# Two arenas of on-chip memory move up by 32 bytes in each partition

## The chip, the cores and the metric

The kernel runs on one core of one Trainium2 chip. The time is device microseconds of one execution, from its own launch to its end. Three runs of the kernel before took 1703.72, 1704.83 and 1706.70 us, a median of 1704.83 us. One further execution was recorded by the hardware profiler; all rows below are of that one.

## The reference

The reference chains two blocks over a sequence of 512 tokens of width 1024, all in 32-bit floats, and returns the normalised stream.

```
def reference(x, c, ctx, ..., g_final_2):
    x = first_block(x, c, ctx, ...)           # modulated norm, 10,240-column projection, 8x64 neighbourhood
                                              # attention with 256 context keys, gated convolution, merge
    return second_block(x, mem_2, ...)        # differential + forget-gate causal attention, memory
                                              # cross attention, squared-ReLU MLP of 4,096, final norm

y_a = (silu(z_a) * b_gate * _dwconv3(c_gate * x_in, conv_w, conv_b)) @ w_out_conv
y_b = (silu(z_b) * attn_o) @ w_out_attn
merged = sigmoid(g_a) * y_a + sigmoid(g_b) * y_b          # then  merged @ w_o
...
a = relu(h @ w1);  (a * a) @ w2                           # the MLP of the second block
```

Almost all arithmetic is matrix products of 1024-wide activations with weight matrices.

## The kernel before, in words

Every weight matrix is cut into jobs of 1,024 x 256 elements (129 of them, 1 MB each). The tensor `raw` holds two jobs as they arrive from memory. ACT copies a job to `wh`, which rounds it to the shortened 32-bit type (fp32r in the rows; `split_hi`, line 314), and DVE or POOL writes what the rounding lost to `wl` (`split_job`, line 320). A product is then three matmuls (`mm3`, lines 438 to 440): high weights with high activations, high with low, low with high. Two such buffers alternate, and the queue of SyncE loads the next job once both parts of the one before last are made.

Activations lie in two arenas, which are two tensors that the whole kernel cuts into views by hand, in KB from the arena's start (`F` and `R`, lines 115 to 120): `farena`, 29.5 KB in each partition, for plain 32-bit values (accumulated results, masks, the residual stream), and `rarena`, 128 KB, for the rounded operands of TensorE in high and low parts. Four further names, `early`, `late`, `upper` and `crown`, are plain 32-bit windows over parts of `rarena`: each is allocated and released again, so that its address stays with the region that `rarena` then takes (lines 93 to 104).

Three kinds of products follow from this. In the usual one (`tiles_job`, `mm3`) a 128x128 piece of `wh` or `wl` is the stationary operand and 512 or 256 columns of `rarena` move through. Where the result is wanted with tokens in the partitions (`token_group`, lines 516 to 518) it is the other way round: a piece of `rarena` is stationary, and 256 columns of `wh` or `wl` move. Where a block product with seven instead of eight multiplications is used (`seven`), the sums of weight quadrants lie in `rarena` too, so that for three of the seven products both operands are in `rarena`; and attention has both operands in the arenas as well. The rows name the moving operand first: `acc<-rarena,wh` moves `rarena` over a stationary `wh`, `acc<-wh,rarena` moves `wh` over a stationary `rarena`, and `acc<-rarena` has both there.

The order of the work is written out by hand engine by engine, with semaphores between them. No planner and no scheduler has a say.

Addresses come from the order of the allocations. The first, `raw`, starts at byte 16,512 of a partition, which is 129 x 128. `raw`, `wh` and `wl` take 16,384 bytes each; `par` 516 bytes, which the allocator rounds up to 544; `ident` and `ones` 512 each; `small` (176 values, line 89) 704. `farena` then starts at 67,936 = 530 x 128 + 96, and, 30,208 = 236 x 128 bytes further, `rarena` at 98,144 = 766 x 128 + 96. All views in the arenas that TensorE reads start a multiple of 256 bytes from the arena's start.

Of the kernel before, what the change touches and what calls it, by code (L numbers as in the profile page):

```python
# [70 lines left out]
def build(nc, A, out):  # L71
# [3 lines left out]
    with ctx:  # L75
        def sb(name, shape, dt=f32):
            return ctx.enter_context(nc.sbuf_tensor(name, shape, dt))
# [8 lines left out]
        par = sb("par", [128, NPAR])  # L86
        ident = sb("ident", [128, 128])
        ones = sb("ones", [128, 128])
        small = sb("small", [128, 176])
        F_KB, R_KB = 29.5, 128  # L90
        farena = sb("farena", [128, int(F_KB * 256)])

# [2725 lines left out]
```

How the kernel before makes its waits and increments, by code:

```python
    def link(self, ins):  # L51
        self.n += 1
        ins.then_inc(self.sem, 1)
        self.eng.wait_ge(self.sem, self.off + self.n)
# [198 lines left out]
        def W(eng, name, value):  # L253
            if not (isinstance(value, int) and value <= 0):
                eng.wait_ge(s_(name), value)
# [11 lines left out]
        def hold(eng, name, value):  # L267
            eng.wait_ge(s_(carried[name][0]), value + carried[name][1])
# [41 lines left out]
        def split_hi(act, it, per, base):  # L310
            s = base % 2
            act.wait_ge(s_(f"raw_loaded{s}"), half(it, per, base) * 16 + 16)
            nc.scalar.activation(wh[:, s], raw[:, s], ACT.Copy).then_inc(s_("hi_done"), 1)
# [1 line left out]
        def split_job(eng, it, per, base):  # L316
            s = base % 2
            eng.wait_ge(s_("hi_done"), job_no(it, per, base) + 1)
            eng.tensor_tensor(wl[:, s], raw[:, s], wh[:, s].bitcast(f32), ALU.subtract)\
               .then_inc(s_("lo_done"), 1)
# [3 lines left out]
        def split_hi_half(act, base, n):  # L325
            s, k = base % 2, slice(4 * n, 4 * n + 4)
            act.wait_ge(s_(f"raw_loaded{s}"), half(0, 2, base) * 16 + 16)
            ins = nc.scalar.activation(wh[:, s, k], raw[:, s, k], ACT.Copy)
            if n == 1:
                ins.then_inc(s_("hi_done"), 1)
# [1 line left out]
        def split_half(eng, base, n):  # L333
            s, k = base % 2, slice(4 * n, 4 * n + 4)
            eng.wait_ge(s_("hi_done"), base + 1)
            ins = eng.tensor_tensor(wl[:, s, k], raw[:, s, k], wh[:, s, k].bitcast(f32), ALU.subtract)
            if n == 1:
```

## Time and profile before

| | us |
|---|---|
| median of three runs | 1704.83 |
| profiled execution, first to last instruction (span) | 1703.5 |
| PE busy in it | 1661.9 (98%) |
| LDWEIGHTS (PEld), beside PE | 1408.0 (83%) |
| DVE busy | 940.9 (55%) |
| ACT busy | 764.6 (45%) |
| POOL busy | 631.7 (37%) |

The profiled execution has no time of its own beside its span; the median of the runs is 1.3 us above it, which holds what lies before the first and behind the last instruction and the difference from run to run. A matmul's length in the rows (0.40 us for 512 columns) is longer than its share of TensorE's time, since successive matmuls overlap: what counts is the step from one start to the next, which the timeline gives.

### The profile page before, as it was taken

What the parts mean: (1) busy time and instruction counts of PE and PEld (TensorE: products, weight loads), DVE (VectorE), ACT (ScalarE), POOL (GpSimd) and SP (SyncE); (2) the same over time, 40 slices, a digit from 0 to 9 for tenths busy, and PEclk for the clock granted to TensorE, in tenths of its full rate; (3) what the DMA queues carried; (4) which work ended last, traced back from release to release, by engine and by line L of the source; (5) the groups of instructions that cost most, each with busy time, mean ns of one, the idle gap of its engine ahead of it and who ended that gap; (6) DMA issues with size and microseconds to landing.
All of it is one profiled execution on the core that took longest, in us unless ns stands there. A gap on an engine that the chain in (4) does not pass through costs nothing. (4 is left out here: it accounts for less than half of the span.)

```text
span 1703.5 us, 26528 instructions
## 1 busy us (share of the span) xinstructions
PE 1661.9 (98%) x10010; PEld 1408.0 (83%) x10010; DVE 940.9 (55%) x1657; ACT 764.6 (45%) x1326; POOL 631.7 (37%) x439
## 2 busy tenths in 40 slices
PE   6999999999999999999999999999999999999998
PEld 4987777778888889978987788798787788989896
DVE  5326566544445258847546664777545565555552
ACT  5324554532223234566545655444445324535351
POOL 1027767342220086643113332965100227323242
PEclk9999999999999999999999999999999999999998
DMA  7322122133333223345632110224411222222221
GB/s 323 112 88 68 55 74 80 63 129 123 106 116 123 99 83 102 105 179 189 233 119 80 50 50 30 96 100 177 169 50 52 98 99 99 100 99 98 99 100 50
DMA packets 29802, 181.68 MB, mean 107 GB/s; under 512 B 3352, under 2 KB 5784, under 8 KB 10112
## 3 DMA queue, kind: packets, MB, share of 16 engines
q1 hardware_dynamic: 22136, 150.12, 24.5%
q10 hardware_dynamic: 7560, 30.09, 5.1%
q8 instruction: 73, 1.20, 0.3%
q14 instruction: 33, 0.27, 0.1%
HBM read 169.57 MB, written 10.50 MB: 106 GB/s over the span
## 5 line engine op out<-in xcount | busy, mean ns | idle before, releaser
L438 PE MATMUL acc<-rarena,wh 128*128 128x512 f32 (+1 forms) x1720 | 657.7, 382 | 6.9 <-DVE rarena L1792 1.3
L440 PE MATMUL acc<-rarena,wl 128*128 128x512 f32 (+1 forms) x1720 | 642.3, 373 | 0.0
L439 PE MATMUL acc<-rarena,wh 128*128 128x512 f32 (+1 forms) x1720 | 641.9, 373 | 0.0
L438 PEld LDWEIGHTS acc<-rarena,wh 128*128 128x128 f32 x1720 | 323.9, 188 | 87.7 <-issue 23.5
L440 PEld LDWEIGHTS acc<-rarena,wl 128*128 128x128 f32 x1720 | 323.8, 188 | 62.1
L439 PEld LDWEIGHTS acc<-rarena,wh 128*128 128x128 f32 x1720 | 324.2, 188 | 56.4 <-issue 0.5
L320 DVE TENSOR_TENSOR wl<-raw,wh 128x2048 fp32r<-128x2048 f32 x81 | 197.2, 2434 | 239.7 <-ACT wh L314 239.6
L314 ACT ACTIVATE wh<-raw 128x2048 fp32r<-128x2048 f32 x99 | 188.9, 1908 | 76.0 <-PE acc L440 69.4
L2555 POOL TENSOR_TENSOR wl<-raw,wh 128x512 fp32r<-128x512 f32 x78 | 105.0, 1375 | 91.2 <-ACT wh L1330 91.2
L320 POOL TENSOR_TENSOR wl<-raw,wh 128x2048 fp32r<-128x2048 f32 x18 | 82.6, 4591 | 149.4 <-ACT wh L314 149.4
L516 PE MATMUL acc<-wh,rarena 128*128 128x256 f32 x336 | 94.2, 280 | 2.7 <-DVE rarena L1792 2.5
L517 PE MATMUL acc<-wl,rarena 128*128 128x256 f32 x336 | 94.1, 280 | 0.0
L518 PE MATMUL acc<-wh,rarena 128*128 128x256 f32 x336 | 94.0, 280 | 0.0
L2610 POOL TENSOR_TENSOR farena<-farena 128x512 f32<-128x512 f32 x34 | 52.4, 1541 | 110.5 <-ACT farena L1646 51.0
L2318 DVE TENSOR_TENSOR farena<-acc,farena 128x512 f32<-128x512 f32 x48 | 33.1, 689 | 89.9 <-PE acc L440 89.7
L1792 DVE TENSOR_TENSOR rarena<-T,rarena 128x512 fp32r<-128x512 f32 (+3 forms) x116 | 64.6, 563 | 23.6 <-ACT rarena L1532 11.1
L1939 DVE CUSTOM_DVE_ANT_1 S<-S,farena 128x512 f32<-128x512 f32 x64 | 43.2, 715 | 59.1 <-PE S L657 59.1
L2542 POOL TENSOR_SCALAR farena<-farena,small 128x256 f32<-128x256 f32 x32 | 32.5, 1036 | 99.9 <-DMA farena<-in_gate 99.9
L2569 POOL TENSOR_TENSOR early<-rarena 128x1024 f32<-128x1024 f32 x8 | 23.0, 2909 | 117.2 <-PE acc L440 117.2
L516 PEld LDWEIGHTS acc<-wh,rarena 128*128 128x128 f32 x336 | 63.3, 188 | 3.5 <-issue 3.2
L2555 POOL TENSOR_TENSOR rarena<-farena,rarena 128x512 fp32r<-128x512 f32 x31 | 41.7, 1345 | 65.0 <-ACT rarena L1728 62.4
L1346 ACT ACTIVATE farena<-farena 128x512 f32<-128x512 f32 x26 | 16.4, 633 | 108.7 <-DVE farena L2075 81.7
(346 smaller groups left out, 3083.2 us busy)
## 6 DMA issues: line engine op xcount, KB each, us to landing
raw<-in_w SPq DMA_DIRECT2D x129, 1024.0 KB, 4.8
early<-in_wmod SPq DMA_DIRECT2D x8, 1024.0 KB, 19.8
farena<-in_gate ACTq DMA_DIRECT2D x4, 1024.0 KB, 4.8
mkv_scratch<-rarena ACTq DMA_DIRECT2D x2, 2048.0 KB, 12.0
rarena<-mkv_scratch ACTq DMA_DIRECT2D x1, 4096.0 KB, 15.0
farena<-in_rpb ACTq DMA_DIRECT2D x16, 240.0 KB, 3.8
farena<-in_x_grid SPq DMA_DIRECT2D x2, 1024.0 KB, 6.9
o_scratch<-early ACTq DMA_DIRECT2D x8, 256.0 KB, 2.0
```

The source lines that it names most:

```text
L314: nc.scalar.activation(wh[:, s], raw[:, s], ACT.Copy).then_inc(s_("hi_done"), 1)
L320: eng.tensor_tensor(wl[:, s], raw[:, s], wh[:, s].bitcast(f32), ALU.subtract)\
L438: mm(o, w[0], m[0], start=start, stop=False)
L439: mm(o, w[0], m[1], start=False, stop=False)
L440: return mm(o, w[1], m[0], start=False, stop=stop)
L516: mm(o, st[0], wh[:, s, k], start=k == 0, stop=False)
L517: mm(o, st[0], wl[:, s, k], start=False, stop=False)
L518: last = mm(o, st[1], wh[:, s, k], start=False, stop=k == KT - 1)
L1792: return tt(dst, src, hi.bitcast(f32), SUB)
L1939: nc.vector.tensor_tensor_reduce(S[a][:], S[a][:], bias, -1.0, 3.0e38, ADD, MIN, negmax[:, cc:cc + 1])\
L2555: return gt(dst, a, b.bitcast(f32), SUB)
L2610: gt(dst, dst, src, ADD).then_inc(s_(name), 1)
```

## The change

One number changes: the tile `small` gets 184 values instead of 176, so 736 bytes instead of 704. No name, view or instruction uses the eight new values. What is allocated behind it moves up by 32 bytes: `farena` to 67,968 = 531 x 128, `rarena` and its four windows to 98,176 = 767 x 128. `raw`, `wh`, `wl`, `par`, `ident`, `ones` and the start of `small` stay. All engines run the same instructions in the same order.

```
@@ -86,7 +86,7 @@
         par = sb("par", [128, NPAR])
         ident = sb("ident", [128, 128])
         ones = sb("ones", [128, 128])
-        small = sb("small", [128, 176])
+        small = sb("small", [128, 184])
         F_KB, R_KB = 29.5, 128
         farena = sb("farena", [128, int(F_KB * 256)])
```

## Rows read from the trace of the kernel before

**Rows 1.** The page's busy time of each engine, its share and count

```profile
PE 1661.9 (98%) x10010; PEld 1408.0 (83%) x10010; DVE 940.9 (55%) x1657; ACT 764.6 (45%) x1326; POOL 631.7 (37%) x439
```

**Rows 2.** Cores: span and mean granted clock

```profile
core 0: 1703.5 us, clock 0.997
```

**Rows 3.** Stretches: length, busy us (count) per engine, clock, DMA share, GB/s

```profile
400.00:445.00 45.00, 45.00 (x195) 36.31 (x194) 19.55 (x24) 12.52 (x12) 13.42 (x11) 1.00 0.35 118
...
850.00:871.00 21.00, 21.00 (x182) 21.00 (x181) 10.07 (x15) 10.18 (x17) 0.00 (x0) 1.00 0.36 126
```

**Rows 4.** Timeline of PE: start us, length us, instruction; 512 columns, 193 steps

```profile
399.92 0.40 PE L438 MATMUL acc<-rarena,wh 128*128 128x512 f32 x1
...
444.95 0.40 PE L439 MATMUL acc<-rarena,wh 128*128 128x512 f32 x1
```

**Rows 5.** Timeline of PE: values of the first block, 149 steps

```profile
54.89 0.28 PE L516 MATMUL acc<-wh,rarena 128*128 128x256 f32 x1
...
72.44 0.28 PE L518 MATMUL acc<-wh,rarena 128*128 128x256 f32 x1
```

**Rows 6.** Timeline of PE: values of the second block, 185 steps

```profile
849.80 0.28 PE L516 MATMUL acc<-wh,rarena 128*128 128x256 f32 x1
...
871.39 0.28 PE L518 MATMUL acc<-wh,rarena 128*128 128x256 f32 x1
```

**Rows 7.** Timeline of PE: first matmul of products of twelve, one job

```profile
661.13 0.29 PE L438 MATMUL S<-rarena 128*128 128x256 f32 x1
...
664.02 0.28 PE L438 MATMUL S<-rarena,wh 128*128 128x256 f32 x1
...
668.28 0.28 PE L438 MATMUL acc<-rarena 128*128 128x256 f32 x1
...
669.71 0.28 PE L438 MATMUL acc<-rarena,wh 128*128 128x256 f32 x1
...
671.13 0.29 PE L438 MATMUL S<-rarena 128*128 128x256 f32 x1
```

**Rows 8.** PE groups by form: busy us, mean ns of one, idle before

```profile
L438 PE MATMUL acc<-rarena,wh 128*128 128x512 f32 x1384 | 560.9, 405 | 3.0 <-ACT farena L1418 1.1 <-DVE farena L1991 0.9 <-DVE wl L320 0.5
...
L438 PE MATMUL acc<-rarena,wh 128*128 128x256 f32 x336 | 96.8, 288 | 3.9 <-DVE rarena L1792 1.3 <-ACT farena L1339 1.1 <-POOL wl L2555 0.9
...
L516 PE MATMUL acc<-wh,rarena 128*128 128x256 f32 x336 | 94.2, 280 | 2.7 <-DVE rarena L1792 2.5 <-DVE rarena L2172 0.2
...
L438 PE MATMUL acc<-rarena 128*128 128x256 f32 x208 | 58.9, 283 | 0.0
...
L438 PE MATMUL S<-rarena,wh 128*128 128x256 f32 x208 | 58.2, 280 | 0.0
...
L438 PE MATMUL S<-rarena 128*128 128x256 f32 x136 | 38.6, 284 | 0.2
```

**Rows 9.** ACT groups by form, 2,048 columns

```profile
L314 ACT ACTIVATE wh<-raw 128x2048 fp32r<-128x2048 f32 x99 | 188.9, 1908 | 76.0 <-PE acc L440 69.4 <-DMA raw<-in_w 2.5 <-issue 2.4
...
L1111 ACT ACTIVATE crown<-farena 128x2048 f32<-128x2048 f32 x3 | 5.7, 1909 | 3.2 <-DMA farena<-in_x_grid 3.2
```

**Rows 10.** DVE groups by form, 512 columns, from a bank of PSUM

```profile
L1792 DVE TENSOR_TENSOR wl<-O,wh 128x512 fp32r<-128x512 f32 x26 | 17.7, 681 | 0.0
L1792 DVE TENSOR_TENSOR rarena<-O,rarena 128x512 fp32r<-128x512 f32 x26 | 17.7, 681 | 0.0
```

**Rows 11.** POOL groups by form, 512 columns

```profile
L2555 POOL TENSOR_TENSOR wl<-raw,wh 128x512 fp32r<-128x512 f32 x78 | 105.0, 1375 | 91.2 <-ACT wh L1330 91.2
...
L2555 POOL TENSOR_TENSOR rarena<-farena,rarena 128x512 fp32r<-128x512 f32 x31 | 41.7, 1345 | 65.0 <-ACT rarena L1728 62.4 <-ACT rarena L1595 1.3 <-ACT rarena L1358 1.3
```

**Rows 12.** DMA issues: queue, count, KB each, median us to landing

```profile
raw<-in_w SPq DMA_DIRECT2D x129, 1024.0 KB, 4.8
...
farena<-in_gate ACTq DMA_DIRECT2D x4, 1024.0 KB, 4.8
```

**Rows 13.** Waits of PE: us in total, times, longest

```profile
PE O L547 <- DMA early<-in_wmod: 12.2, 1, 12.2
```

More of the change, by code:

```diff
@@ L88, in build @@
         ones = sb("ones", [128, 128])
-        small = sb("small", [128, 176])
+        small = sb("small", [128, 184])
         F_KB, R_KB = 29.5, 128
```

## Prediction

> **What bounds the kernel now.** I read the busy times first. PE works in 1661.9 of 1703.5 us and no other engine in more than 55% [rows 1], so all other work together keeps TensorE waiting for 41.6 us. The clock comes next: granted at 0.997 of full speed over the span [rows 2], and at 1.00 with PE busy throughout in long stretches [rows 3], which is its upper level of 2.4 GHz. TensorE is therefore neither starved nor slowed, and the time is the sum of its steps.
>
> Third, the step itself, from one matmul's start to the next. With 512 columns moving from `rarena` over weights in `wh` or `wl`, 193 steps take 444.95 - 399.92 = 45.03 us, 233.3 ns each [rows 4]. With 256 columns moving from `wh` or `wl` over a stationary piece of `rarena`, 185 steps of the second block take 21.59 us, 116.7 ns each [rows 6], and 149 steps of the first block 17.55 us, 117.8 ns each [rows 5]. In a seven-product job both other pairings stand side by side, twelve matmuls to a product [rows 7]: 661.13 to 664.02 is two products and 668.28 to 669.71 one product with both operands in `rarena`, 4.32 us for 36 steps or 120.0 ns; 664.02 to 668.28 and 669.71 to 671.13 are four products of `rarena` over `wh` or `wl`, 5.68 us for 48 steps or 118.3 ns.
>
> Last, how many of each there are; each line of the product helpers stands for one of three like groups [rows 8]. 512 columns: 3 x 1384 = 4152. 256 columns of `rarena` over `wh` or `wl`: 3 x (336 + 208) = 1632. 256 columns of `wh` or `wl` over `rarena`: 3 x 336 = 1008. Both in `rarena`: 3 x (208 + 136) = 1032. By their steps these are 4152 x 233.3 ns = 969 us, 193 us, 118 us and 124 us, together some 1404 of the 1662 us. One nanosecond more or less in each of these 7,824 steps is 7.8 us: so only a change of the step could move the time.
>
> **The change part by part.** No instruction, wait, transfer or order changes. Two things do: the arenas start at 0 instead of 96 past a multiple of 128 bytes, and, because `wh` and `wl` already start at 0, an operand in an arena and one in `wh` now stand at equal places within 128 bytes, where they stood 96 apart. What each engine could gain is read from pairs of rows that do like work in `raw`, `wh`, `wl` (at 0) and in the arenas (at 96).
>
> ACT: 2,048 columns from `raw` to `wh` take 1908 ns, from `farena` to `crown` 1909 ns [rows 9]. DVE: 512 columns of a PSUM bank minus the high part take 681 ns to and from `wl` and `wh` as to and from `rarena` [rows 10]. POOL: 1375 ns there, 1345 ns here [rows 11], the arena being no worse. DMA: a load of 1,024 KB into `raw` lands in 4.8 us, one into `farena` in 4.8 us [rows 12]. So all four terms are zero. If I am wrong on these, PE covers them: their durations reach the end only through its 41.6 idle us, and the one large piece of that, 12.2 us, is the first matmuls waiting for the loads of the modulation weights into `early` [rows 13], a transfer of the kind that rows 12 show equal.
>
> PE: no row shows a matmul with both operands in 128-byte step, so its cost has to be bounded from the pairings that there are.
>
> - The end of a gain. Suppose the differences above are the price of an operand at 96: 118.3 - 116.7 = 1.6 ns where the moving one is, 120.0 - 118.3 = 1.7 ns where the stationary one is. All would go: (4152 + 1632) x 1.6 = 9.3 us, 1008 x 1.7 = 1.7 us, 1032 x 3.3 = 3.4 us, 14.4 us in all.
> - The end of a loss. Suppose instead that the 120.0 ns is the price of two operands at equal places, which only the pairs inside `rarena` have now. All would pay it: 1008 x 3.3 = 3.3 us, 1632 x 1.7 = 2.8 us, and 4152 x 1.7 = 7.1 us if the wide ones do too, 13.2 us in all.
>
> I take zero, for two reasons. The values of the first and the second block are the same pairing with the same places within 128 bytes, and yet they differ by 1.1 ns (117.8 and 116.7) [rows 5, 6]; differences of this size therefore arise without any difference in place. And 512 columns that move from 96 cost 233.3 ns, while two times 256 columns that move from 0 cost 233.4 ns [rows 4, 6]: a moving operand off the multiple costs nothing per column.
>
> The sum is 1703.5 us of the profiled span plus zero. The median of the runs lies 1.3 us above that span, and since it is a run's time that is forecast, I predict the median: 1704.8 us.
>
> **Rivals.**
>
> *The place itself costs.* The end of the gain, 1704.8 - 14.4 = 1690.4 us; if only the 256-column forms, whose differences are rows, follow it, (1632 x 1.6 + 1.7 + 3.4) = 7.7 us and 1697.1 us. For it speaks that the three pairings order themselves as it wants (116.7, 118.3, 120.0). Against it: 117.8 for the same places as 116.7, and the wide step above.
>
> *Equal places collide.* This is the slower one. While a matmul streams, the next stationary operand is loaded (PEld is busy 83% of the span beside PE [rows 1]); were two streams at equal places within 128 bytes to meet more often, products over `wh` in the seven-product jobs would step at 120.0 ns. It decides as soon as these leave 118.3 ns. Its price is 3.3 + 2.8 = 6.1 us for the 256-column forms, 1710.9 us, and 1718.0 us with the wide ones. For it: only the equal pairs are at 120.0 now. Against it: they are also the only ones with both operands in one tensor, and the two streams advance at different rates, so that where they start ought to matter little.
>
> *The surplus over the clock goes.* At 2.4 GHz 512 columns would be 213.3 ns and 256 columns 106.7 ns; the steps have 20.0 ns and 10.0 to 13.3 ns more. Every one of the 7,824 matmuls has at least one operand at 96, so the trace has no direct counterexample. If all of it went: 4152 x 20.0 + 1632 x 11.6 + 1008 x 10.0 + 1032 x 13.3 = 126 us, 1579 us. Against it: the surplus grows with the columns (10.0 for 256, 20.0 for 512), and those that move from 0 have it per column like those that move from 96; a stationary operand of always 128 columns can't cost in proportion to what moves.
>
> The Trainium skill (TensorE: Matmul & The Clock Gate, Back-to-back issue gap) gives a warm step of N/2.4 + 2.5 ns for a lone stream, 215.8 ns for 512 columns. The trace has 233.3, so the measurement decides; by that rule, if the missing 17.5 ns were the arenas' place, 4152 wide steps would give back 72.7 us by an estimate from that page.
>
> **How the numbers follow.** Two medians of this kernel closer than about 0.2%, 3.4 us, can't be told apart. No change: 0.76, 1701.4 to 1708.2. The place itself costs: 0.10. Equal places collide: 0.09. The surplus goes: 0.02. The rest, 0.03, is a shift of the measurement beyond 0.2% either way. That makes 0.13 for faster, 0.76 for the same, 0.11 for slower. The range reaches to the two middle rivals at the prices that rows show, with the 256-column forms alone: 1697 to 1711. Their full ends, 1690.4 and 1718.0, and the surplus are left out, as at most 1 in 10 together.
>
> **What would show it.** Right: steps of 233.3, 116.7 to 117.8, 118.3 and 120.0 ns in the same four places, 1908, 681 and 1345 ns for the three engines in the arenas, and a span within 3.4 us. The place: wide steps under 232 ns and the three 256-column pairings drawn together towards 116.7. Collision: the products over `wh` at 120.0 ns, and wide steps near 235. Wrong in another way: steps as before, but a span that moves by more than 3.4 us, with the difference in PE's 41.6 idle us.

## The result and the profile after

The changed kernel took 1686.06 us (median of four runs, 1685.4 to 1689.24) beside 1704.91 us for the kernel before (four runs). The ratio is 0.9893 [0.988, 0.9906]: it is 1.1% faster, where no change was forecast, and it lies outside the range of 1697 to 1711.

The profiled execution took 1686.52 us. First its busy times and its core's row (columns as in [rows 1, 2]).

```profile
PE 1643.3 (98%) x10010; PEld 1410.8 (84%) x10010; DVE 941.8 (56%) x1657; ACT 764.6 (45%) x1326; POOL 631.6 (37%) x439
core 0: 1684.7 us, clock 0.996
```

The span is 18.8 us shorter and PE is busy 18.6 us less. Its idle time is 1684.7 - 1643.3 = 41.4 us, as it was 41.6 [rows 1], and the granted clock is 0.996 beside 0.997 [rows 2]. So TensorE's own steps became shorter. The timeline of PE has them, in the places that rows 4 to 7 show: 512 columns of `rarena` over `wh` or `wl` (first and last of 197 rows), then the values of the first block (156 rows) and of the second (170 rows).

```profile
399.67 0.39 PE L440 MATMUL acc<-rarena,wl 128*128 128x512 f32 x1
...
444.09 0.39 PE L438 MATMUL acc<-rarena,wh 128*128 128x512 f32 x1
...
54.32 0.28 PE L517 MATMUL acc<-wl,rarena 128*128 128x256 f32 x1
...
72.92 0.28 PE L516 MATMUL acc<-wh,rarena 128*128 128x256 f32 x1
...
839.72 0.28 PE L516 MATMUL acc<-wh,rarena 128*128 128x256 f32 x1
...
860.00 0.28 PE L517 MATMUL acc<-wl,rarena 128*128 128x256 f32 x1
```

The wide form: 44.42 us for 196 steps, 226.6 ns, where it was 233.3 [rows 4]. The values: 18.60 us for 155 steps and 20.28 us for 169, 120.0 ns in both blocks, where they were 117.8 [rows 5] and 116.7 [rows 6]. And the seven-product job, twelve matmuls from one row to the next:

```profile
656.97 0.28 PE L438 MATMUL acc<-rarena 128*128 128x256 f32 x1
...
658.41 0.28 PE L438 MATMUL acc<-rarena,wh 128*128 128x256 f32 x1
...
659.85 0.28 PE L438 MATMUL S<-rarena 128*128 128x256 f32 x1
...
661.29 0.28 PE L438 MATMUL acc<-rarena 128*128 128x256 f32 x1
...
662.73 0.28 PE L438 MATMUL S<-rarena,wh 128*128 128x256 f32 x1
```

Every product takes 1.44 us, 120.0 ns a step, whether over `wh` (118.3 before) or with both operands in `rarena` (120.0 before) [rows 7]. So all four pairings moved to two values: the wide form down by 6.7 ns, the three forms of 256 columns up to 120.0 or left there. The stretch of the wide rows shows the other conditions unchanged: PE without a gap, the clock at its upper level of 2.4 GHz (columns as in [rows 3]).

```profile
400.00:445.00 45.00, 45.00 (x200) 37.25 (x199) 20.92 (x23) 12.59 (x13) 13.24 (x11) 1.00 0.33 117
```

The rows of the other engines answer to [rows 9 to 13] one by one: ACT 1908 and 1909 ns, DVE 681 and 681, POOL 1348 (1345 before), the loads 4.8 and 4.9 us, the longest wait for the modulation weights 11.6 us (12.2 before).

```profile
L314 ACT ACTIVATE wh<-raw 128x2048 fp32r<-128x2048 f32 x99 | 188.9, 1908 | 73.1 <-PE acc L440 66.5 <-DMA raw<-in_w 2.5 <-issue 2.3
...
L1111 ACT ACTIVATE crown<-farena 128x2048 f32<-128x2048 f32 x3 | 5.7, 1909 | 2.6 <-DMA farena<-in_x_grid 2.6
...
L2555 POOL TENSOR_TENSOR rarena<-farena,rarena 128x512 fp32r<-128x512 f32 x31 | 41.8, 1348 | 65.9 <-ACT rarena L1728 63.3 <-ACT rarena L1595 1.3 <-ACT rarena L1358 1.3
...
L1792 DVE TENSOR_TENSOR rarena<-O,rarena 128x512 fp32r<-128x512 f32 x26 | 17.7, 681 | 0.0
L1792 DVE TENSOR_TENSOR wl<-O,wh 128x512 fp32r<-128x512 f32 x26 | 17.7, 681 | 0.0
...
raw<-in_w SPq DMA_DIRECT2D x129, 1024.0 KB, 4.8
...
farena<-in_gate ACTq DMA_DIRECT2D x4, 1024.0 KB, 4.9
...
PE O L547 <- DMA early<-in_wmod: 12.9, 2, 11.6
```

Adding up, form by form, the time from each matmul's start to the next in both traces accounts for 18.2 of the 18.8 us. "Without a gap" are steps that last under 300 ns (512 columns) or under 150 ns (256) in both traces; the last column has all steps of a form, the longer ones too:

| form | steps without a gap | mean before, after (ns) | us |
|---|---|---|---|
| 512 columns, `rarena` over `wh`/`wl` | 3,986 | 233.4, 227.8 | -21.1 (-22.1 without a gap, +1.0 in the longer ones) |
| 256 columns, `wh`/`wl` over `rarena` | 1,139 | 117.2, 119.9 | +2.7 |
| 256 columns, `rarena` over `wh`/`wl` | 1,596 | 118.4, 119.9 | +2.0 |
| 256 columns, both in `rarena` | 1,128 | 119.7, 119.8 | -0.2 |
| first products over the modulation weights | | | -1.1 |
| all others | | | -0.5 |

The change is a gain of the wide form and a smaller loss of two others.

### The profile page after: what moved, and what is told of

Same layout as the page of the kernel before. It is cut to its first block and busy times, and to the rows that moved or that the text cites. A ratio compares the mean times of both kernels' runs of the same rounds, so it can differ in the third digit from the quotient of the medians.

```text
span 1684.7 us, 26528 instructions
## 1 busy us (share of the span) xinstructions
PE 1643.3 (98%) x10010; PEld 1410.8 (84%) x10010; DVE 941.8 (56%) x1657; ACT 764.6 (45%) x1326; POOL 631.6 (37%) x439
## 5 line engine op out<-in xcount | busy, mean ns | idle before, releaser
L438 PE MATMUL acc<-rarena,wh 128*128 128x512 f32 (+1 forms) x1720 | 650.9, 378 | 6.8 <-ACT farena L1613 1.3
L440 PE MATMUL acc<-rarena,wl 128*128 128x512 f32 (+1 forms) x1720 | 634.6, 369 | 0.0
L439 PE MATMUL acc<-rarena,wh 128*128 128x512 f32 (+1 forms) x1720 | 634.6, 369 | 0.0
L314 ACT ACTIVATE wh<-raw 128x2048 fp32r<-128x2048 f32 x99 | 188.9, 1908 | 73.1 <-PE acc L440 66.5
L2542 POOL TENSOR_SCALAR farena<-farena,small 128x256 f32<-128x256 f32 x32 | 36.0, 1146 | 96.0 <-DMA farena<-in_gate 96.0
L2555 POOL TENSOR_TENSOR rarena<-farena,rarena 128x512 fp32r<-128x512 f32 x31 | 41.8, 1348 | 65.9 <-ACT rarena L1728 63.3
```

The lines of the kernel that those rows point to most:

```text
L314: nc.scalar.activation(wh[:, s], raw[:, s], ACT.Copy).then_inc(s_("hi_done"), 1)
L438: mm(o, w[0], m[0], start=start, stop=False)
L439: mm(o, w[0], m[1], start=False, stop=False)
L440: return mm(o, w[1], m[0], start=False, stop=stop)
L2555: return gt(dst, a, b.bitcast(f32), SUB)
```

## Experiments

The theories after the result. **Distance**: a step depends on how far apart in bytes the moving operand and the stationary operand lie; the stationary operand of the next matmul is loaded while this one streams. **Place**: each operand pays by itself for not starting at a multiple of 128. **Another engine**: the arenas' place speeds up ACT, DVE, POOL or a DMA, and TensorE gains through them. "Distance" below is the start of the operand in the arena (or its stand-in) less that of the weights, in bytes modulo 256; successive stationary pieces lie a multiple of 512 bytes apart, so that it is one number for a form of products. It is 224 before and 0 after; where both operands lie in `rarena`, it is 0 in both kernels. Edits are shown against the kernel before, and "..." stands for lines left out.

**m1_steps.** TensorE alone, 48 matmuls to a setting, each over another stationary piece:

```
for r in range(RUN):
    m0, s0 = r % (4096 // n) * n + ms // 4, r % 32 * 128 + ss // 4
    emit(acc[b][0:c, 0:n], sta[:, s0:s0 + c], mov[:, m0:m0 + n], r == 0, r == RUN - 1)
```

> This kernel is not the reference's computation: it copies the input into two rounded tensors, a moving and a stationary one, and runs 48 matmuls for each of 41 settings of the two operands' places within 128 bytes and of their widths; its output is the input. Theory 'equal places' (the step depends on the difference of the two places): with 128 stationary columns and a difference of 0, 226.7 ns for 512 columns and 120.0 ns for 256, at any common place (32, 64, 96 as well as 0), and 233.3 ns and 117 to 118 ns at a difference of 96 or 32, whichever operand is moved. Theory 'each by itself' (an operand off a multiple of 128 costs): 226.7 ns for 512 columns only where both are at 0, 233.3 ns at common places of 32, 64 or 96. If the 13.3 ns over the clock at a difference of 0 are the loading of the stationary columns, 64 columns leave 6.7 ns and 32 columns 3.3 ns, so 220.0 and 216.7 ns for 512 columns. If only the start within a line of 16 bytes counts, all settings are alike but the last two (4 and 8 bytes).

With `ms` and `ss` at 0 the two tensors happen to lie 128 bytes apart, so the distance is 128 + `ms` - `ss`. In the timeline of PE a setting is one merged row (start, length, count); its step is the length less that of one matmul (0.39 or 0.40 us) over the count less one. Moving operand 96 bytes on (distance 224); 112 bytes on (240); stationary operand alone 112 bytes on (16); both 96 bytes on (128):

```profile
97.30 9.73 PE L80 MATMUL acc<-mov,sta 128*128 128x512 f32 x41
...
108.47 9.68 PE L80 MATMUL acc<-mov,sta 128*128 128x512 f32 x42
...
231.50 9.46 PE L82 MATMUL acc<-mov,sta 128*128 128x512 f32 x41
...
264.83 9.72 PE L83 MATMUL acc<-mov,sta 128*128 128x512 f32 x41
```

That is 233.4, 226.7, 226.7 and 233.4 ns. No other engine is at work, so the effect is TensorE's own. Moving the stationary operand alone changes the step of the stream as moving the streamed one does, and moving both by 32, 64 or 96 leaves it at 233.4 (232.2 unmoved). Both theories had expected 226.7 ns with both operands at 0, and that of equal places at the common places too; m2_map shows why it didn't come: a distance of 128 isn't one of 0. Of the other settings: with 256 columns the steps ran from 113.3 to 120.0 ns over the distances; 32 stationary columns instead of 128 gave 113.3 for 120.0 ns with 256 columns, but 230.5 for 232.2 and, once settled, 240.0 for 233.4 with 512, so that a smaller load isn't simply cheaper. Four bytes off gave 240.0 ns.

**e1_all_at_32.** Distance against place: everything at 32 past a multiple of 128, distances as in the changed kernel.

```
+        front = sb("front", [128, 8])
...
-        small = sb("small", [128, 176])
+        small = sb("small", [128, 184])
```

> The arenas and raw, wh and wl all lie 32 bytes past a multiple of 128, so nothing that was at 0 in the changed kernel is at 0 here, but their places are equal as there. Theory 'equal places': steps of 226.7 ns (512 columns) and 120.0 ns (256), a time of 1686 us as the changed kernel. Theory 'each by itself': 233.3 ns and a time of 1705 us or more, since now all operands are off.

1686.79 us, ratio 0.9907 [0.9891, 0.9924]. The wide form's timeline, first and last of 196 rows, has 44.20 us for 195 steps, 226.7 ns:

```profile
399.63 0.39 PE L441 MATMUL acc<-rarena,wl 128*128 128x512 f32 x1
...
443.83 0.39 PE L441 MATMUL acc<-rarena,wl 128*128 128x512 f32 x1
```

The whole gain is there with no operand at a multiple of 128. Place falls.

**e2_only_rarena.** `farena` stays at 96, only `rarena` and its windows move.

```
         farena = sb("farena", [128, int(F_KB * 256)])
+        gap = sb("gap", [128, 8])
```

> farena stays at 96 as before, only rarena and its windows move to 0. If TensorE's operands are the whole cause: 226.7 and 120.0 ns and 1686 to 1687 us. If the plain arena (evictions, masks, the stream, its transfers) has a part: some us of the 18.9 stay behind, the more the larger that part; all of it would leave 1705 us.

1685.12 us, ratio 0.9892 [0.9876, 0.9909]; first and last of 195 rows, 43.98 us for 194 steps, 226.7 ns:

```profile
399.80 0.39 PE L439 MATMUL acc<-rarena,wh 128*128 128x512 f32 x1
...
443.78 0.39 PE L441 MATMUL acc<-rarena,wl 128*128 128x512 f32 x1
```

`farena`, which only other engines and DMAs use beside TensorE's transposes and some small products, adds nothing: what gains lies in `rarena` and its windows. Other engines use these too; that they gain nothing there is shown by their rows after the change, and that TensorE gains by itself by the runs with TensorE alone.

**e4_at_64.** Another multiple: distance 64, arenas at 64 past a multiple of 128.

```
-        small = sb("small", [128, 176])
+        small = sb("small", [128, 200])
```

> Both arenas lie at 64 instead of 0 past a multiple of 128, wh and wl at 0. If what has to be equal is the place within 64 bytes: steps of 226.7 and 120.0 ns and 1686 us. If it is the place within 128 bytes: steps as before, 233.3 and 117 to 118 ns, and 1705 us, or a step of its own between the two.

1687.42 us, ratio 0.9896 [0.9871, 0.992]; first and last of 194 rows, 44.17 us for 193 steps, 228.9 ns:

```profile
399.75 0.39 PE L440 MATMUL acc<-rarena,wl 128*128 128x512 f32 x1
...
443.92 0.39 PE L438 MATMUL acc<-rarena,wh 128*128 128x512 f32 x1
```

A gain as large with the arenas off a multiple of 128. It is made up otherwise: the wide form gains less (13.8 us by the same account), and 256 columns of `rarena` over `wh` fall to 115.2 ns on average, a gain of 3.5 us where the change loses 2.0. That average is of no single step: the form goes at 117.7 ns in some stretches (680.19 to 684.43 us) and at 113.3 in others (690.10 to 692.82 us, the same products of the next job). The values do the same, 117.8 ns in the first block and 113.3 from 823 to 862 us in the second. So one distance can have two steps in one kernel. Its four runs lie between 1681.97 and 1690.81, so it can't be told from the changed kernel; whether other stretches took the shorter step in the faster runs, which have no trace, isn't shown.

**m2_map.** TensorE alone in the kernel's own order of three matmuls (high over high, high over low, low over high), every distance.

```
for k in range(KT):
    for n, (hi, lo) in enumerate(((0, 0), (0, 1), (1, 0))):
        last = f(acc[(b + t) % 2], x, t, k, hi, lo, ...)
```

> Not the reference's computation: TensorE alone, in the kernel's own pattern of three matmuls (high over high, high over low, low over high) for two column pieces and eight slices, 48 matmuls for each distance between the arena's start and the weights' start, 0 to 240 bytes in steps of 16; 'wide' moves 512 columns of the arena over the weights, 'half' 256 of them, 'turn' 256 columns of weights over a piece of the arena. No other engine works beside it. Theory 'distance' (the step depends on the distance of the two operands alone, with nothing of the other engines in it): wide 226.7 ns at 0 and 128, 233.3 at 96 and 224, 229 to 230 at 64 and 192; half 120.0, 118.3, 114 to 115; turn 120.0, 117, 116. If the other engines' traffic makes the surplus: 215 to 216 ns at every distance. If the distance counts modulo 256 and not 128, 128 to 240 differ from 0 to 112.

Steps in ns, good to about 0.3; "half" moves 256 columns of the arena's stand-in over the weights, "turn" moves 256 columns of weights over it:

| distance | wide | half | turn | | distance | wide | half | turn |
|---|---|---|---|---|---|---|---|---|
| 0 | 226.7 | 119.8 | 120.0 | | 128 | 232.3 | 118.4 | 118.6 |
| 16 | 231.6 | 118.7 | 118.4 | | 144 | 233.3 | 118.7 | 120.0 |
| 32 | 233.3 | 116.6 | 118.4 | | 160 | 234.3 | 117.3 | 119.7 |
| 48 | 233.4 | 118.3 | 117.8 | | 176 | 233.3 | 119.3 | 118.1 |
| 64 | 229.1 | 117.8 | 113.3 | | 192 | 233.4 | 113.4 | 113.3 |
| 80 | 231.1 | 119.9 | 118.7 | | 208 | 234.7 | 119.3 | 116.6 |
| 96 | 233.5 | 120.0 | 118.7 | | 224 | 233.4 | 118.3 | 116.8 |
| 112 | 231.1 | 113.3 | 120.0 | | 240 | 226.7 | 117.2 | 119.9 |

The merged rows of wide at 0, at 224 and at 240, of half at 0 (length of one 0.28) and of turn at 64:

```profile
36.71 9.68 PE L60 MATMUL acc<-mov,sta 128*128 128x512 f32 x42
...
192.78 9.73 PE L60 MATMUL acc<-mov,sta 128*128 128x512 f32 x41
...
203.95 9.46 PE L60 MATMUL acc<-mov,sta 128*128 128x512 f32 x41
...
269.69 5.32 PE L63 MATMUL acc<-mov,sta 128*128 128x256 f32 x43
...
383.01 5.04 PE L66 MATMUL acc<-sta,mov 128*128 128x256 f32 x43
```

Row 224 of the table is the kernel before (233.3, 118.3, and 116.7 in the second block, with 117.8 in the first) and row 0 the kernel after (226.6, 120.0, 120.0). Wide at 256, 288, 320, 352 and 384 gave 227.2, 233.4, 228.9, 233.6 and 233.4, those of 0 to 128 within 1.1: the distance counts modulo 256, and not modulo 128, since 0 and 128 differ by 5.6 ns; the expectation of like steps at 0 and 128, and at 64 and 192, is a miss. Not all of the map agrees with m1_steps: at 16 that run has 226.7 where the map has 231.6, and at 112 it has 233.3 for 231.1. The distance is therefore not everything at each place of the table.

**e5_at_32.** Does the map hold in the kernel where it forecasts no gain?

```
-        small = sb("small", [128, 176])
+        small = sb("small", [128, 192])
```

> Arenas at 32, weights at 0. Theory 'distance', with the sign counting: a step of its own, which m2 gives at 32. If only its size counts (32 before or behind is alike): as before, 233.3, 117 to 118.3 ns and 1703 to 1705 us. If each operand wants a multiple of 128 by itself: the same 1703 to 1705 us.

1705.33 us, ratio 1.0 [0.9988, 1.0012]; first and last of 190 rows, 44.10 us for 189 steps, 233.3 ns; half and turn at 117.1 and 118.3.

```profile
399.76 0.39 PE L438 MATMUL acc<-rarena,wh 128*128 128x512 f32 x1
...
443.86 0.40 PE L438 MATMUL acc<-rarena,wh 128*128 128x512 f32 x1
```

As the map has it to 0.5 ns, though the theory of place expects no gain here either. Beside e1, this also shows the arenas at 32 both with the gain (weights at 32 too) and without it (weights at 0).

**e6_mlp_64, e6_mlp_192.** The map's best wide step is at 0 and its best 256-column steps are elsewhere. So both at once: the changed kernel with the operand of the MLP's seven-product jobs 64 or 192 bytes further.

```
-        xc = view(rarena, 96, (8, 4, 256)), view(rarena, 64, (8, 4, 256))
+        xc = view(rarena, 96 + 0.0625, (8, 4, 256)), view(rarena, 64 + 0.0625, (8, 4, 256))
...
```

> The changed kernel with the MLP's block operands (xc, and the plain window late that it is made from) 64 bytes further, the rest at a distance of 0; farena is trimmed by 512 unused bytes to make room. The 12 seven-product jobs of the MLP have 576 matmuls of xc over weights and 432 of xc over sums in rarena, all 120.0 ns in the changed kernel. Theory 'distance': the first step at about 115 ns as in the run with the arenas at 64, the second at 113 to 118, all else (226.7 ns wide) as in the changed kernel: 576 x 4.8 + 432 x 4.5 = 4.7 us less, about 1681.5 us. Theory 'a multiple of 128 for each': these steps get worse or stay, 1686 us or more.

> The same with 192 bytes. Theory 'distance modulo 256': 113.4 ns as the map shows at 192, for both pairings: (576 + 432) x 6.6 = 6.7 us less than the changed kernel, about 1679.5 us. If the distance counted modulo 128: the same as with 64 bytes.

1687.49 us, ratio 0.9905 [0.989, 0.992], and 1685.2 us, 0.9891 [0.9876, 0.9906]: both as the changed kernel. In e6_mlp_64, three products of such a job, 36 steps:

```profile
1506.43 0.28 PE L438 MATMUL S<-rarena 128*128 128x256 f32 x1
...
1510.67 0.28 PE L438 MATMUL acc<-rarena,wh 128*128 128x256 f32 x1
```

4.24 us, 117.8 ns for 120.0, which is the map's value for half at 64 and not the 115 expected from e4. In e6_mlp_192 the same products go at 117.8, too, where the map has 113.4, until the last job: there, behind two steps of 252 and 193 ns near 1620 us, they go at 113.3. Two stretches of e6_mlp_192, 120 steps and 72:

```profile
1600.39 0.28 PE L438 MATMUL acc<-rarena,wh 128*128 128x256 f32 x1
...
1614.52 0.28 PE L438 MATMUL S<-rarena,wh 128*128 128x256 f32 x1
...
1621.54 0.28 PE L438 MATMUL acc<-rarena,wh 128*128 128x256 f32 x1
...
1629.70 0.28 PE L438 MATMUL acc<-rarena 128*128 128x256 f32 x1
```

That is 14.13 us and 8.16 us, 117.8 and 113.3 ns. The distances are the same in both, and jobs with either weight buffer went at 117.8 before, so what ran before decides here, and the map's value is one of two. The time moved by nothing that can be told: a miss. The map can't simply be carried over to a stream that is entered in another way.

**e7_at_240.** The map's other fast wide distance: all views in `rarena` 16 bytes further than before.

```
-            ap = arena[:, int(kb * 256):int(kb * 256) + n]
+            at = int(kb * 256) + (0 if arena is farena else 4)
+            ap = arena[:, at:at + n]
...
```

> rarena and its windows start at 112 past a multiple of 128 (a distance of 240, or -16, from the weights modulo 256), farena at 96 as before: nothing in the arenas lies on a multiple of 128 or even of 32 bytes. Theory 'distance': the map's 226.7 ns wide, 117.2 half, 119.9 turn, so 1632 x 2.7 = 4.4 us less than the changed kernel, about 1682 us. Theory 'a multiple of 128 for each': 1704 us or more.

1713.95 us, ratio 1.0049 [1.0033, 1.0066]: slower. First and last of 188 rows, 44.26 us for 187 steps, 236.7 ns, where the map has 226.7:

```profile
399.63 0.40 PE L441 MATMUL acc<-rarena,wl 128*128 128x512 f32 x1
...
443.89 0.40 PE L439 MATMUL acc<-rarena,wh 128*128 128x512 f32 x1
```

The largest miss, and the reason for the last run. This kernel has a second step, too: from 1193 to 1231 us, as from 1101 to 1116, the wide form goes at 233.3 ns. First and last of 145 rows there, 33.60 us for 144 steps:

```profile
1193.31 0.39 PE L440 MATMUL acc<-rarena,wh 128*128 128x512 f32 x1
...
1226.91 0.39 PE L440 MATMUL acc<-rarena,wh 128*128 128x512 f32 x1
```

**m3_far.** The map's order of three again, wide form only, at the kernel's distance of 65,264 bytes and the map's 33,008 (both 240), with other banks, pauses and work beside.

```
for name, dist, bank, slot, pause, load in plan():
    if pause:
        n += 1
        last.then_inc(go, 1)
        pe.wait_ge(back, n)
    last = run(dist, bank, slot)
```

> TensorE alone again; the output is its input. All products are of the wide form, 512 columns, in the kernel's own order of three, 48 matmuls to a setting. The map with TensorE alone gave 226.7 ns at a distance of 240 bytes modulo 512, the whole kernel shifted to that distance gave 236.65 ns. What differed: the kernel's moving tensor lies 65,264 bytes behind the weights and the map's 33,008 (both 240 modulo 512); what ran on TensorE before; other banks of results; other engines at work beside. Here each is changed by itself, with 224 (233.4) and 256 (226.7) as the two settings known from both. Theory A, higher address bits decide: 236.65 ns at the far distance and 226.7 at the near one, whatever ran before, and the ten settings with distances 240 + 512j between tell which bit. Theory B, the step locks to what ran before: the same distance gives 226.7 in one place of the sequence and 236.65 in another, above all after a pause. Theory C, other engines' traffic: 226.7 in all quiet settings, 236.65 only in those beside which ACT and DVE work. Theory D, none of these: 226.7 in all settings at 240, and the reason for the kernel's 236.65 stays open. At 224 all theories expect 233.4 and at 0 or 256 226.7 ns in every setting; A leaves open that these too change with higher bits.

Far at 256; far at 240; near at 240 behind a pause of 2 us; far at 256 behind such a pause; far at 256 with ACT and DVE at work:

```profile
50.83 9.46 PE L114 MATMUL acc<-mov,sta 128*128 128x512 f32 x41
...
61.74 9.96 PE L114 MATMUL acc<-mov,sta 128*128 128x512 f32 x42
...
291.25 10.10 PE L114 MATMUL acc<-mov,sta 128*128 128x512 f32 x42
...
304.86 9.48 PE L114 MATMUL acc<-mov,sta 128*128 128x512 f32 x41
...
508.19 9.68 PE L114 MATMUL acc<-mov,sta 128*128 128x512 f32 x42
```

By these rows, to about 0.3 ns, 226.7, 233.3, 236.7, 227.1 (226.7 once settled) and 226.7 ns. At 240 all twenty settings that follow another without a pause give 233.3, near and far, whatever the higher address bits, the bank or the weight slot: theory A falls. Work beside changes nothing at 0, 224, 240 or 256, though ACT and DVE are busy 7.87 and 7.90 of 8 us there (busy of PE, PEld, DVE, ACT, POOL):

```profile
509.00:517.00 8.00, 8.00 (x37) 6.63 (x36) 7.90 (x4) 7.87 (x5) 0.00 (x0) 1.00 0.01 2
```

So theory C falls. Behind two of three pauses the step at 240 settles at 236.7, which is the kernel's main value, and the map and m1_steps had 226.7: three lasting steps at one distance. That m3_far has two of them in one run, as e7 has within one kernel, is theory B for 240. At 0 and 256 all twelve settings come to 226.7, and at 224 all nine to 233.3, as in both kernels. So the two distances of this change showed one step each in the wide form, and 240 three. What picks one of them stays open: behind the other pause the same distance went on at 233.3, and the map and the eighth setting here both came to 240 from 224, one with 226.7 and one with 233.3. The two runs were on different chips, and nothing separates that from what ran earlier.

## Why the prediction was wrong

The step that failed is the sentence "a moving operand off the multiple costs nothing per column", and with it "I take zero". It set 512 columns that move from 96 beside two times 256 that move from 0. That a place by itself has no price is even true (e1). But the comparison changed which operand lay at 96 and kept the two 32 bytes apart in both rows; the distance, the one thing that decides here, was never varied in it. With it varied, 233.4 becomes 226.7 [m2_map, e1_all_at_32]. The equality of 233.3 and 233.4 was luck besides: with the first block's 117.8 ns two times 256 columns come to 235.6, and a step isn't proportional to its columns (m1_steps at 224: 111.7, 118.4, 173.4 and 233.3 ns for 128, 256, 384 and 512).

Point by point:

- That only a change of the step could move the time, and that ACT, DVE, POOL and DMA terms are zero: right, by the rows after and by e2_only_rarena.
- The end of a gain, 1.6 ns a step: the mechanism (place) is refuted by e1, and e4 gains with the arenas off a multiple; e5 can't tell, since place and distance both expect no gain there. The term for the 4,152 wide steps, 6.6 us, was mis-sized: the wide form gave 21.1 us. No row before bounds it, since no wide product of that kernel had another distance. The range took the ends of the 256-column forms for ends of everything.
- "Equal places collide": its number came for 256 columns, where the products over `wh` left 118.3 for the 120.0 ns it named, and the values too (+2.0 and +2.7 us of the 2.8 and 3.3 forecast). Its mechanism isn't borne out: in the map places equal within 128 bytes (a distance of 128) give 118.4 and 118.6 ns (m1_steps has 120.0), and unequal ones (80 and 96 for half, 112 and 144 for turn) give about 120.0. It was wrong in carrying 1.7 ns to the wide form, which went the other way. The only equal pairs in the trace were of 256 columns, both in `rarena`; the sentence that no row shows a matmul with both operands in 128-byte step overlooks them.
- "The two streams advance at different rates, so that where they start ought to matter little": refuted by e5_at_32 and e1_all_at_32, where moving the weights alone takes the wide step from 233.3 to 226.7 ns, and by m1_steps.
- "The surplus over the clock goes" got 0.02, because the surplus grew with the columns, 10 and 20 ns. After the change it is 226.7 - 213.3 = 13.3 ns and 120.0 - 106.7 = 13.3 ns. A third of the wide form's surplus was a matter of distance, and its growth with the columns held at the distance of 224 and doesn't at 0.
- Two like values, 117.8 and 116.7, were taken as the size of chance differences. They are now both 120.0. That one pairing can have two lasting steps at one distance is what e6_mlp_192, e7 and m3_far show, and in e4 these same two blocks stand at 117.8 and 113.3. So it is right that such differences arise without one in place, but they put no bound on what another distance does.

The Trainium skill (TensorE: Matmul & The Clock Gate, Step-by-step: what each phase is for) tells of two independent read ports, one for the stream and one for the weights being loaded, so that the load takes no read bandwidth from the stream. The runs show that the two are not independent in time, at least for these 4-byte operands with a load to each matmul: 233.3 against 226.7 ns by the stationary operand's place alone (e5_at_32, e1_all_at_32). Whether they meet at these ports or elsewhere was not measured; the runs show the dependence, not the circuit.

That both arenas now start at a multiple of 128 bytes isn't what gains: `rarena` alone does it, and a common shift off the multiple keeps it.

## What to carry to other kernels

Where TensorE's steps set the time, vary the pad ahead of an arena by 16 or 32 bytes and read the step of every form of product: it follows the distance between moving and stationary operand and, at some distances, what ran before; one form's gain is another's loss, and the net here was 1.1%. To judge an address change from a trace, compare pairs of operands that differ in their distance; rows that differ only in which operand is off a multiple say nothing on it. A map made with TensorE alone carried over at 0, 32 and 224; at 64 (256 columns) and for the MLP's operand at 192 the kernel had the map's value only in some stretches, and at 240 it never had the wide one. So the kernel itself has the last word, and a mean over it may hide two steps.

## What the runs showed of the hardware

- With 128 stationary columns, a weight load to each matmul and starts at multiples of 16 bytes, the step of 512 columns lies between 226.7 and 236.7 ns at the upper clock, and that of 256 columns between 113.3 and about 120. Addresses alone make 6.7 ns of it (e5_at_32 against e1_all_at_32).
- At some distances the step is not one number: 226.7, 233.3 and 236.7 ns for 512 columns at 240, 117.8 and 113.3 ns for 256 columns at 64 (e4_at_64) and at 192 (e6_mlp_192), each steady over tens of matmuls or more.
- At the lower clock of 1.2 GHz no surplus is left at the distance that was caught there, 240. In m3_far, behind the first pause, the clock row and two nested rows of the timeline:

```profile
276.00:278.50 2.50, 2.50 (x7) 1.97 (x6) 0.00 (x0) 0.00 (x0) 0.00 (x0) 0.50 0.00 0
```

```profile
275.76 1.32 PE L114 MATMUL acc<-mov,sta 128*128 128x512 f32 x3
...
275.76 3.03 PE L114 MATMUL acc<-mov,sta 128*128 128x512 f32 x7
```

Granted 0.50, and 1.71 us for four steps more, 427 ns, which is 512 columns at 1.2 GHz with no surplus.
